# Where an expert's rows lie among its 64 places: rank r at place r, or at place 8 (r mod 8) + r div 8

## The reference

```
g_idx = argmax(h @ w_rg + b_rg)             # one of 4 groups
e_top, e_idx = top_k(logits[group], 2)      # two of its 8 experts
gate = g_p * softmax(e_top)
y[token] += gate * ((silu(x @ w_gate[e]) * (x @ w_up[e])) @ w_down[e])   # D=1024, D_EXPERT=256
out = rmsnorm_2(x + y)
```

```
 0-15: 44 50 40 25 15 34 20 12 28 14 21 24 21 25 32 29
16-31: 89 43 53 51 35 47 40 14  7 30 37 29 11 31 48 25
```

## Time and profile before

| | us |
|---|---|
| three timed runs | 1327.51, 1327.68, 1330.31; median 1327.68 |
| the profiled execution's own time | 1328.05 |
| its span, on which all rows below stand | 1325.9 |
| PE, DVE, ACT, POOL busy | 1249.1, 611.8, 460.1, 530.7 |
| moved from and to HBM | 205.76 MB read, 16.78 MB written |

### The profile page before, as it was taken

How to read it: one execution, slowest core, us unless ns; L and a number is a source line. 1 busy time by engine, 2 the same in 40 slices (tenths; PEclk the granted TensorE clock), 3 DMA queues, 4 the chain that set the end, 5 groups by cost and what they waited for, 6 DMA issues and landing times.

```text
span 1325.9 us, 17097 instructions
## 1 busy us (share of the span) xinstructions
PE 1249.1 (94%) x5986; PEld 921.5 (69%) x5986; DVE 611.8 (46%) x1121; ACT 460.1 (35%) x767; POOL 530.7 (40%) x681
## 2 busy tenths in 40 slices
PE   6999999999999999999999999999999599898794
PEld 4767777778888888888888788777888444333342
DVE  4868768626542422222227765564352442222116
ACT  5657543445444233142245434254223100000002
POOL 4644323235655645545556637336453101111100
PEclk9999999999999999999999999999999789999998
DMA  6422212122343434334333334213339689999984
GB/s 210 112 64 62 66 48 65 49 64 79 95 110 104 135 89 134 96 96 127 96 95 111 95 80 112 64 49 111 93 117 378 224 339 421 424 424 426 425 372 199
DMA packets 210998, 214.23 MB, mean 162 GB/s; under 512 B 31435, under 2 KB 192957, under 8 KB 198260
## 3 DMA queue, kind: packets, MB, share of 16 engines
q1 hardware_dynamic: 201856, 203.14, 45.3%
q0 software_dynamic: 4752, 8.10, 1.7%
q10 hardware_dynamic: 4324, 2.12, 0.5%
HBM read 205.76 MB, written 16.78 MB: 168 GB/s over the span
## 4 chain that ended last, share of the span: by engine, by line
issue 38%; POOL 31%; PE 25%; DVE 3%; ACT 1%; POOLq 0%; DMA 0%; DVEq 0%; ACTq 0%
POOL wlo L595 31%; PE bank L2070 9%; PE bank L2087 5%; PE bank L1717 3%; PE bank L1719 3%; PE bank L1718 3%; PE side L1747 1%; ACT hid L1016 1%; DVE hid L1570 1%; PE side L1719 1%; PE side L1718 1%; PE side L1717 1%; PE bank L2155 1%; PE side L1998 1%; ACT hidT L1019 0%
## 5 line engine op out<-in xcount | busy, mean ns | idle before, releaser
L595 POOL TENSOR_TENSOR wlo<-raw,whi 128x256 fp32r<-128x256 f32 x644 | 497.1, 803 | 526.8 <-ACT whi L699 526.6
L1718 PE MATMUL bank<-actB_lo,whi 128*128 128x512 f32 x608 | 237.0, 390 | 0.0
L1717 PE MATMUL bank<-actB_hi,whi 128*128 128x512 f32 x576 | 227.9, 396 | 0.5 <-POOL wlo L595 0.5
L1719 PE MATMUL bank<-actB_hi,wlo 128*128 128x512 f32 x576 | 224.6, 390 | 0.0
L699 ACT ACTIVATE whi<-raw 128x1024 fp32r<-128x1024 f32 x161 | 169.0, 1051 | 150.3 <-PE bank L1719 124.9
L1717 PE MATMUL bank<-actA_hi,whi 128*128 128x512 f32 x400 | 157.1, 393 | 1.7 <-DVE actA_lo L1099 1.6
L1719 PE MATMUL bank<-actA_hi,wlo 128*128 128x512 f32 x400 | 155.9, 390 | 0.0
L1718 PE MATMUL bank<-actA_lo,whi 128*128 128x512 f32 x400 | 155.9, 390 | 0.0
L1718 PEld LDWEIGHTS bank<-actB_lo,whi 128*128 128x128 f32 x608 | 114.3, 188 | 24.1 <-issue 1.0
L2070 PE MATMUL bank<-gu,xeT 128*64 128x512 f32 x496 | 120.1, 620 | 9.1 <-issue 7.6
L1717 PEld LDWEIGHTS bank<-actB_hi,whi 128*128 128x128 f32 x576 | 108.2, 188 | 25.5 <-issue 2.3
(11 more groups left out here) (379 smaller groups left out, 1622.6 us busy)
## 6 DMA issues: line engine op xcount, KB each, us to landing
gu<-in_w_exp_gate SPq DMA_DIRECT2D x33, 1024.0 KB, 18.4
gu<-in_w_exp_up SPq DMA_DIRECT2D x33, 1024.0 KB, 20.8
dn<-in_w_exp_down SPq DMA_DIRECT2D x33, 1024.0 KB, 23.9
raw<-in_w_in SPq DMA_DIRECT2D x57, 512.0 KB, 3.9
raw<-in_w_up SPq DMA_DIRECT2D x32, 512.0 KB, 3.9
raw<-in_w_down SPq DMA_DIRECT2D x32, 512.0 KB, 3.9
raw<-in_w_out SPq DMA_DIRECT2D x16, 512.0 KB, 4.0
raw<-in_w_in SPq DMA_DIRECT2D x16, 256.0 KB, 3.2
```

The lines of the kernel that those rows point to most:

```text
L595: ins = nc.gpsimd.tensor_tensor(wlo[:, slot, at], raw[:, slot, at], whi[:, slot, at].bitcast(F32), ALU.subtract)
L1717: mm(b[:, :], w_hi, hi[:, k, :], start=first, stop=False)
L1718: mm(b[:, :], w_hi, lo[:, k, :], start=False, stop=False)
L1719: ins = mm(b[:, :], w_lo, hi[:, k, :], start=False, stop=last)
```

## The change

Rank r stands no longer at place r, but at place 8 (r mod 8) + r div 8. The ranks 0, 1, 2, ... 7 are at the places 0, 8, 16, ... 56, the ranks 8 to 15 at 1, 9, 17 and so on. `at_row` is still written in order of the places; the row numbers against which it compares are now read with a step of 8 elements. The number of rows, transfers, instructions and waits is as before, and the order of instructions on each engine too. An expert with 32 rows filled the places 0 to 31 before; now it fills the first four of every eight.

```diff
-            rows64 = const("iota")[:, 0:ROWS]
+
+            rows64 = const("iota")[:, 0:ROWS].rearrange("p (a b) -> p b a", a=8)
+
+            def by_place(x):
+                return x.rearrange("p t (b a) -> p t b a", a=8)
+
             for k in range(2):
                 eight = slice(NT * k, NT * (k + 1))
-                chain(v.tensor_tensor(at_row[:, eight, :], rows64.unsqueeze(1).broadcast_to([P, NT, ROWS]),
-                                      pos[:, eight].unsqueeze(2).broadcast_to([P, NT, ROWS]), ALU.is_equal), S("picks_placed"))
+                chain(v.tensor_tensor(by_place(at_row[:, eight, :]), rows64.unsqueeze(1).broadcast_to([P, NT, 8, 8]),
+                                      pos[:, eight].unsqueeze(2).unsqueeze(3).broadcast_to([P, NT, 8, 8]), ALU.is_equal),
+                      S("picks_placed"))
...
-                chain(v.tensor_tensor(at_row[:, :, :], rows64.unsqueeze(1).broadcast_to([P, 2 * NT, ROWS]),
-                                      every(pos[:, :], ROWS), ALU.is_equal))
+                chain(v.tensor_tensor(by_place(at_row[:, :, :]), rows64.unsqueeze(1).broadcast_to([P, 2 * NT, 8, 8]),
+                                      pos[:, :].unsqueeze(2).unsqueeze(3).broadcast_to([P, 2 * NT, 8, 8]), ALU.is_equal))
```

## The result

| | median of the timed runs (lowest to highest) | profiled span |
|---|---|---|
| before | 1328.69 us (1327.51 to 1330.61), 5 runs | 1325.9 |
| after | 1334.56 us (1334.31 to 1335.35), 5 runs | 1332.3 |

The ratio is 1.0044, 95% interval [1.0032, 1.0055]. I had predicted 4.2 us more, and measured are 5.9 more (6.4 between the two profiled spans).

What follows compares the result with a forecast made beforehand. The stage was taken as bound by its slowest DMA engine, through the landing of unit 14's weights. Rows (3.9 us) plus the stepped read (0.3 us) put the median at 1331.9 us, range 1329.0 to 1335.2.

Steps and rivals of the forecast that it cites:

- the split in fours: Gathers and scatters: places 0-3 and 32-35 share one DMA engine, eight engines per half; rival splits eights and sixteenths 3% each.
- 25 rows x 0.154 = 3.86 us: Hottest DMA engine up to unit 14's weights: 163 rows instead of 138, so those weights land 3.86 us later.
- the last time it was idle (about 1089 ...): Start of the row count: the hottest DMA engine was taken as last idle at about 1089, before unit 4's weights landed.
- part 1: Gathers and scatters: extra rows on the hottest DMA engine delay unit 14's weights by 3.86 us, with nothing covering it.
- 3.9 + 0.3: Sum of the delays: 3.9 us for rows on the hottest engine, 0.3 us for reading row numbers with a step; 65%.
- The read in steps: VectorE's two comparisons ahead of the first gather get slower by 0.3 us in all, delaying the whole stage, DMA included.
- The waits: TensorE's waits for weights: a new one of some 2.4 us before unit 11; unit 12 at 1231.0, unit 14 at 1264.7.
- Behind unit 14: After unit 14's start the hottest engine's last load is 3.4 us later, TensorE 3.9; slack grows to 1.8 us, costing nothing.
- The fall of the DMA share: At the end, every other engine finishes early: share falls to about a half and stays, 11.7 us mean idle against 8.3.
- The clock: Rival: TensorE's slow clock behind the wait before unit 14 is spared (1329.1, 7%) or lasts twice as long (1334.7, 10%).
- the main case: Whole kernel: 3.9 us for rows plus 0.3 us for the stepped read, giving 1331.9 us within 1.5 us; 65%.
- the clock's high end: Rival: TensorE's slow clock behind the wait before unit 14 lasts twice as long, giving 1334.7 us; 10%.

Runs made afterwards that it cites:

- spread: Kernel before with an expert's rows dealt in turn to its eight DMA engines, ranks read from a constant table: 1323.09 us, ratio 0.9955.
- odd: Kernel before with the change's placement moved to the other four engines of each half, ranks from a constant table: 1334.74 us, ratio 1.0043.
- old_old: Kernel before, same placement, plus the machinery of two rank tables (extra VectorE operations ahead of the first list): 1333.30 us.
- table_after: Kernel before with the change's placement, row numbers from a ready constant table read without a step: 1335.06 us, ratio 1.0047.
- unit4_new: Against old_old: the same two-table machinery, with the change's placement for experts 8 and 9 (unit 4) alone: 1336.43 us.
- before_gain_late: Kernel before with the 512 KB load of the norm's gains moved behind the last weight load: 1328.94 us, ratio 0.9996.
- blocks: Kernel before with each engine's eight places filled before the next engine's, ranks from a constant table: 1338.94 us, ratio 1.0073.

## Why the prediction was right in its direction and small in its size

1. *What bounds the stage, and the split in fours.* Right. The engine with most rows sets the landing; four placements came out in the order of its rows, on both sides of the kernel before. The rule of the Trainium skill (DMA: Bandwidth & Descriptors, "The descriptor swizzle") that I had found to agree with the table holds for these gathers and scatters: spread, built on it, gained 5.6 us where 32 rows x 0.154 say 4.9, and the events of the single engines lie as it says.
2. *25 rows x 0.154 = 3.86 us.* Right as the price of the rows: behind the first batch, where 23 of the 25 fall and make 3.5 us, 3.4 to 3.9 us in the traces of that placement and of odd.
3. *The step that failed* is the start of that count, "the last time it was idle (about 1089 ...)": I took it that from there on only bytes count, whatever the placement. The first batch is longer in all traces with the change's placement in unit 4: by 2.1 to 2.6 us against old_old, by 3.0 us in table_after against before, and rows explain under 1 of it. So the term of part 1 was mis-sized: the start of unit 14 moved by 6.75 us where I had 3.9 + 0.3, since one or a few DMA engines fall behind at the start of that count, for a reason that stays open. In the medians, less than in single traces, what is missing is 5.9 - 4.2 = 1.7 us.
4. *The read in steps.* 0.63 us each where I had said 0.5 to 0.6, 0.4 us for both; unit 0's first product of `gate_up` moves from 1063.86 to 1064.10, 0.24 us. The size was right. That it "delays the whole stage, DMA with it" is not shown: unit 4's first weight load is issued 0.2 us earlier than before (from trace to trace this moment moves by over 1 us), and table_after shows that the term can't be seen in the total.
5. *The waits.* A wait before unit 11 of some 2.4 us: 2.95, and one before unit 10 as well. Unit 12 at 1231.0: 1232.62. Unit 14 at 1264.7: 1267.29. The stretch from 12 to 13: 16.47 us (1249.09 - 1232.62), as predicted. From 13 to 14: 18.20 and not 17.3; in table_after and odd, with equally many rows, it is 17.5 and 17.6, so some 0.6 us of this belongs to that one trace.
6. *Behind unit 14.* No more is lost, as predicted: the span grows by 6.4, unit 14's start by 6.75. The slack of the last down weights is 1.4 us (1.3 before, predicted 1.8).
7. *The fall of the DMA share.* "Early to about a half", and there it stays (0.51, 0.52, 0.50): right. From 1278 to the landing at 1303.5 the engines are idle for some 10.6 us in the mean, predicted were 11.7. That is (-0.01 + 0.30 + 0.49 + 0.48 + 0.50 + 0.64) x 4 = 9.6, and 0.69 x 1.5 = 1.0.
8. *The clock.* The two long products took 9.61 and 9.35 us, together 0.5 more than before, and unit 14's, the one on the path, 0.3 less; it is not what made the difference. So it is luck that the range held: 1334.56 lies beyond the main case (1331.9 within 1.5 us) and inside the range only by the room that I had given to the clock's high end (1334.7). Of the 2.7 us above 1331.9, 1.0 is the kernel before itself, whose median was 1328.69 here and 1327.68 when I predicted.

## What to carry to other kernels

A load is there when the most burdened DMA engine is done, so where a stage is bound by DMA, count the bytes of the fullest engine and not their total: here 25 rows of 4 KB on one engine, among 61 loads of 1 MB, cost some 4 us, while the total of bytes stayed the same. With indirect transfers of 128 partitions, deal the filled places out in turn to the groups of four partitions (spread: place 32c + 4b + a holds rank 32c + 8a + b), and not every eighth place first, which looks even by place and loads every other engine; and where the engines run dry ahead of a long busy stretch, a single engine can start it some microseconds late, which a count of bytes doesn't give: look at the events of the 16 engines for that batch, in several traces.

## What was not expected of the hardware

- Right after a stretch in which the DMA engines were partly idle (share 0.51 to 0.60 in a window of 2 us) one of the 16 can be 1.6 us late with its 64 KB of the first load and over 3 us late four loads on, while the other 15 keep the times of the kernel before (unit4_new, before_gain_late).
- In blocks they moved 360 and 332 GB/s in two windows of 2 us there at a share of 0.94 and 1.01, and 426 and 430 in the same windows of the kernel before; later in the stage that one moves 424 to 426.
- The first batch of loads after it lands 18.5 to 19.6 us or 21.3 to 22.6 us after its first issue, never between, and the longer of SP's two issues of unit 4's down weights takes 1.0 to 1.8 us in the second case (1408 ns in the rows above), 0.65 us at most in the first.
